# One row tile ahead of the expert rows instead of two: the order of a streaming encoder layer with gathered experts

## The reference, cut to what matters

```
h    = RMSNorm(x);  proj = h @ w_in            # 5416 columns: aq ak av, index, bq bk bv, 4 x 512 gate columns
oA   = attention over the top-k keys of an indexer;  oB = attention in a band with a bias
x    = x + (sig(gA) * (oA @ w_br_a) + sig(gB) * (oB @ w_br_b)) @ w_out
q    = RMSNorm(x) @ w_pq                       # 8 heads, two half keys each, against 128 + 128 centroids
e, g = 16 of 16384 experts per head and token, with softmax weights: 128 expert slots per token
x    = x + sum_k g_k * gelu(u[e_k] . h) * v[e_k]     # u, v: 16384 x 1024 (67 MB each)
```

## Time and profile before

| | before |
|---|---|
| time, median of 3 | 1466.76 us (1457.18 to 1469.15) |
| the profiled execution's own time | 1468.48 us |
| its span, first to last instruction | 1466.7 us |
| mean granted clock of TensorE | 0.841 of 2.4 GHz |
| busy: PE, DVE, ACT, POOL | 1168.0, 991.4, 294.8, 653.9 us |
| DMA moved | 434.92 MB |

### The profile page before, as it was taken

One profiled execution on the slowest core, in us unless ns is written; L12 is line 12 of the kernel. 1 busy time (PEld: TensorE's weight loads), 2 busy tenths in 40 slices (PEclk: granted clock), 3 DMA queues, 4 the chain that ended last, 5 costly groups with the idle time before them and its releaser, 6 DMA issues.

```text
span 1466.7 us, 12558 instructions
## 1 busy us (share of the span) xinstructions
PE 1168.0 (80%) x4129; PEld 695.6 (47%) x4129; DVE 991.4 (68%) x2233; ACT 294.8 (20%) x703; POOL 653.9 (45%) x565
## 2 busy tenths in 40 slices
PE   7999999798455664745778654277999999999998
PEld 3544544685125664635345654265444444444443
DVE  2526322487849998788768999998565666666662
ACT  2014631111000102111244643397000000000000
POOL 1220000265555556577646645556545454444450
PEclk9999999899775555555898876567999999999999
DMA  7643522398997778789999877676999999999994
GB/s 284 212 157 125 186 80 92 133 379 318 339 385 243 254 265 300 259 277 342 355 348 378 300 252 259 218 234 216 401 410 409 409 405 409 410 409 409 409 409 183
DMA packets 155362, 434.92 MB, mean 297 GB/s; under 512 B 14592, under 2 KB 36496, under 8 KB 155040
## 3 DMA queue, kind: packets, MB, share of 16 engines
q0 software_dynamic: 74688, 271.66, 50.7%
q1 hardware_dynamic: 80608, 162.45, 30.2%
HBM read 427.72 MB, written 6.34 MB: 296 GB/s over the span
## 4 chain that ended last, share of the span: by engine, by line
PE 57%; DVE 18%; DMA 11%; ACT 6%; another core or an unknown queue 4%; issue 2%; POOL 0%; SPq 0%; DVEq 0%; ACTq 0%
PE wide L1213 30%; PE accumB L896 8%; DVE rows_ring L1546 8%; PE accumA L896 5%; DMA arena<-in_w_in 3%; ACT hot L828 2%; PE wide L1103 2%; PE accumB L1125 2%; DVE arena L1534 2%; DMA ring<-in_w_in 2%; PE accumB L1159 1%; ACT hot L831 1%; DMA ring<-in_w_pq 1%; PE transB L1159 1%
## 5 line engine op out<-in xcount | busy, mean ns | idle before, releaser
L595 POOL DMA_INDIRECT rows_ring<-in_peer_u,expert x384 | 485.7, 1265 | 358.6 <-DVE dots L1546 277.6
L1546 DVE CUSTOM_DVE_ANT_0 rows_ring<-rows_ring,arena 128x1024 f32<-128x1024 f32 x384 | 459.3, 1223 | 108.3 <-DMA rows_ring<-in_peer_u,expert 105.4
L1213 PE MATMUL wide<-ring,arena 128*128 128x512 f32 x1024 | 441.9, 594 | 0.7 <-issue 0.7
L1213 PEld LDWEIGHTS wide<-ring,arena 128*128 128x128 f32 x1024 | 195.3, 191 | 246.8 <-issue 246.8
L1551 DVE SCALAR_TENSOR_TENSOR x<-rows_ring,dots,x 128x1024 f32<-128x1024 f32 x128 | 164.4, 1285 | 97.2 <-DMA rows_ring<-in_peer_v,expert 97.2
L595 POOL DMA_INDIRECT rows_ring<-in_peer_v,expert x128 | 125.1, 977 | 136.6 <-DVE x L1551 125.7
L872 PE MATMUL transB<-ident,arena 128*128 128x128 f32 x198 | 49.1, 392 | 81.4 <-DVE arena L1405 28.7
L896 PE MATMUL accumB<-arena 128*128 128x512 f32 x160 | 79.5, 654 | 26.0 <-DMA arena<-in_w_in 25.3
L896 PE MATMUL accumB<-ring,arena 128*128 128x512 f32 (+1 forms) x192 | 83.0, 587 | 12.3 <-DMA ring<-in_w_in 9.5
L828 ACT ACTIVATE hot<-iota,turned 128x128 f32<-128x128 f32 x256 | 81.0, 390 | 5.7 <-DVE expert L1504 5.7
L535 POOL TENSOR_SCALAR ssx<-ssx 128x1 f32<-128x1 f32 x6 | 2.0, 335 | 176.7 <-ACT arena L615 176.7
(11 more groups left out here) (215 smaller groups left out, 1376.5 us busy)
## 6 DMA issues: line engine op xcount, KB each, us to landing
ring<-in_peer_v SPq DMA_DIRECT2D x128, 512.0 KB
ring<-in_w_in SPq DMA_DIRECT2D x10, 2048.0 KB
arena<-in_w_in SPq DMA_DIRECT2D x10, 2048.0 KB
ring<-in_w_pq SPq DMA_DIRECT2D x4, 2048.0 KB
arena<-in_w_pq SPq DMA_DIRECT2D x4, 2048.0 KB
arena<-in_w_out SPq DMA_DIRECT2D x3, 2048.0 KB, 14.0
rows_ring<-in_peer_u,expert POOLq DMA_INDIRECT x384
arena<-in_w_br_a SPq DMA_DIRECT2D x2, 2048.0 KB
```

Source lines behind the costliest of these rows:

```text
L595: pool.indirect_dma_start(rowbuf[:, n % ROWS, :], None, u_rows if n < U_ROWS else v_rows, index).then_inc(S(f"rows{n % ROWS}"), 16)
L1213: ins = pe.matmul(wide[:, 2 * t + half, :], dense[t][:, b, :], vblock[:, b % VBLOCKS, half * 512:half * 512 + 512], start=b == 0, stop=b = ...
L1546: v.tensor_tensor_reduce(row, row, h2[:, t, :], 1.0, 0.0, ALU.mult, ALU.add, dots[:, t, k:k + 1]).then_inc(S("row_used"), 1)
```

## The change

The two Groups become three Lanes: A (tile 0, "first"), B (tile 1, "second") and C (sample). Ahead of the rows only lane A runs: projection, attention, gates, branches, output, queries (tables FIRST_*, in `before_rows`). Tiles 1 and 2 are projected together as a group GL ("late") between rows, from position 0.5 on; then B's attention, gates, branches, output and queries run between rows at positions 5 to 31, beside C's. Weights are thus loaded in three passes where there were two: the seven projection groups for A and for GL, the gates, branches, output and query weights for each of A, B and C. A's pass uses four ring slots, the others two. B has one transpose bank and one sum bank (transA, accumA), C the other two.

The dense matrix is laid out by token (`[p, token, block]`), so that a group of four tokens fills 512 contiguous floats, and ORDER names the sequence in which tile 0's groups are put, so that each goes where the arena is free already. In the last loop the stationary operand is now `dense[t][:, :, b]`, whose elements lie 128 floats (512 bytes) apart.

```
-PROJ = [4.5, 5.5, 6.5, 7.5, 8.5, 9.5, 10.5]
-GATES = [40.5, 41.5, 43, 44]
-AT = dict(heads_a=14, index=15, select=19.5, score_a=[18.5, 20.5, 21.5, 22.5], soft_a=24.5, values_a=[26.5, 27, 27.5, 28],
-          heads_b=25.5, score_b=[28.5, 30, 31.5, 33], soft_b=36, values_b=[38, 38.5, 39, 39.5], branch=[46, 47.5], merge=49,
-          out=[49.5, 51], scale=52, h2=53)
-QUERY = dict(prompt=[-8, -4, -3, -2, -1], sample=[53, 56, 59, 62])
-ROUTE = [[[-7, -7, -5, -5, -3, -3, 0]] + [route_at(2, 4), route_at(6), route_at(13.5)], [route_at(m) for m in (16.5, 21, 28.5, 42.5)],
-         [route_at(m) for m in (56, 59, 62, 65)]]
-DENSE = [(35, 46, 1.7), (67, 67.5, 4)]
+FIRST_PROJ = [9, 14, 21, 28, 35, 42, 49]
+FIRST_AT = dict(index_heads=27, index=34, heads_a=41, select=38, score_a=[48], soft_a=52, values_a=[57, 57, 57, 57],
+                heads_b=61, score_b=[70], soft_b=71, values_b=[87, 87, 87, 87], gates=[62, 71, 80, 98], branch=[91, 105],
+                merge=112, out=[114, 121], scale=130, h2=131, late=78, centroids=48.5, h_late=24)
+LATE_PROJ = [0.5, 1.5, 3, 4.5, 5.5, 7, 8.5]
+SECOND_AT = dict(index_heads=5, index=6, heads_a=7, select=7.5, score_a=[8], soft_a=9.5, values_a=[12.5, 13, 13, 13.5],
+                 heads_b=11.5, score_b=[12.5], soft_b=13.5, values_b=[15.5, 16, 16, 16.5],
+                 gates=[10, 11, 14, 14.5], branch=[17, 18.5], merge=20, out=[20.5, 22], scale=23.5, h2=24)
+SAMPLE_AT = dict(index_heads=5.5, heads_a=12, index=16.5, select=21, score_a=[21.5, 22.5, 23.5, 24], soft_a=26,
+                 values_a=[27.5, 28, 28.5, 29], heads_b=26.5, score_b=[29.5, 31, 32.5, 34], soft_b=36.5,
+                 values_b=[39.5, 40, 40, 40.5], gates=[33, 34.5, 36, 37], branch=[42, 43.5], merge=45, out=[46, 47.5],
+                 scale=49, h2=50)
+QUERY = dict(first=[-8, -4, -3, -2], second=[25, 27, 29, 31], sample=[50.5, 53, 55.5, 58])
+         [route_at(m) for m in (27.5, 31, 34.5, 39.5)],
+         [route_at(m) for m in (52.5, 55.5, 58.5, 61.5)]]
+DENSE = [(35, 44, 1.8), (64.5, 65, 4)]
+ORDER = [[28, 29, 30, 31] + list(range(8)) + list(range(12, 20)) + list(range(8, 12)) + [20, 21, 27] + list(range(22, 27)),
+         list(range(TGROUPS))]
...
+        LOADS = [("first", name, n % 4) for n, name in enumerate(NAMES7 + REST)]
+        LOADS += [("late", name, n % 2) for n, name in enumerate(NAMES7)]
+        LOADS += [(owner, name, (n + 1) % 2) for owner in ("second", "sample") for n, name in enumerate(REST)]
...
-                    act.activation(dense[t][:, :, g * TOKENS:g * TOKENS + TOKENS],
-                                   built[(g + 1) % 2][:, :].rearrange("p (n b) -> p b n", n=TOKENS),
+                    act.activation(dense[t][:, first:first + TOKENS, :],
+                                   built[(g + 1) % 2][:, :].rearrange("p (n b) -> p n b", n=TOKENS),
                                    ACT.Copy).then_inc(S("dense_put"), 1)
...
-            between = [laid(x) for x in (early(steps(G0)), queries(G0), steps(G1), dense_weights(0), queries(G1),
-                                         dense_weights(1))]
+            before_rows([laid(x) for x in (project(GF, FIRST_PROJ), attention(A), gates(A), finish(A))])
+            between = [laid(x) for x in (queries(A), project(GL, LATE_PROJ), attention(B), gates(B), finish(B),
+                                         attention(C), gates(C), finish(C), queries(B), dense_weights(0), queries(C),
+                                         dense_weights(1))]
...
-                        ins = pe.matmul(wide[:, 2 * t + half, :], dense[t][:, b, :],
+                        ins = pe.matmul(wide[:, 2 * t + half, :], dense[t][:, :, b],
                                         vblock[:, b % VBLOCKS, half * 512:half * 512 + 512],
```

More of the change, by code:

```diff
@@ L367, in laid @@
                 m = yield
-        def early(steps):
-            for k in steps:
-                yield FIRST if k >= 0 else k
         def start_laid(between):
@@ new lines, in _ @@
+            sp.wait_ge(to(GL, "h_ready"), 2)
+            sp.dma_start(gain[:, :], to_all_rows(i["g_ffn"])).then_inc(S("gain_in"), 16)
+            for n in range(4):
+                weights("first", f"pq{n}")
+            for name in ("ix", "aq"):
+                weights("late", name)
+            sp.wait_ge(to(A, "query_done"), 16)
+            sp.wait_ge(to(A, "score_done"), 4)
+            sp.dma_start(cik, i["cache_a_ik"][0].rearrange("b k d -> k b d")).then_inc(S("cik_in"), 16)
+            for name in ("ak", "av", "bq", "bk", "bv"):
+                weights("late", name)
@@ new lines, in gate_copies @@
+            def gate_copies(L):
+                for n, at in enumerate(AT[L.name]["gates"]):
+                    yield at + 0.5
+                    act.wait_ge(to(L, "gate_done"), n + 1)
+                    if L is C and n == 0:
+                        act.wait_ge(to(C, "logits_read"), 1)
+                        act.wait_ge(S("state_stored"), 16 * 15)
+                    bank = {"first": [sumB, sumB, sumA, sumA], "second": [sumA] * 4, "sample": [sumB] * 4}[L.name][n]
+                    act.activation(L.gates[:, n * 512:n * 512 + 512], bank, ACT.Sigmoid).then_inc(to(L, "gate_copied"), 1)
@@ L747, in steps @@
-                if G is G1:
-                    yield from groups(range(7, NG), [p + 1 for p in GATES])
-                yield AT["merge"]
-                for t in every:
-                    for half in range(2):
-                        copy_rows(G, "merged", t, half)
-                for t in every:
-                    yield LAST["out"] if t else AT["scale"]
-                    act.wait_ge(to(G, "x1_added"), 2 * t + 2)
-                    squares(G.tiles[t], 1)
-                    yield LAST["out"] if t else AT["h2"]
-                    for half in range(2):
-                        copy_rows(G, "h2", t, half)
@@ new lines, in finish @@
+            def finish(L):
+                at = AT[L.name]
+                for br in range(2):
+                    yield at["branch"][br]
+                    branch(L, br)
+                yield at["merge"]
+                pe.wait_ge(to(L, "merged_ready"), 1)
+                rows(L, "merged", L.merged)
+                for n in range(2):
+                    yield at["out"][n]
+                    weights_wait(pe, L.name, f"out{n}")
+                    if n == 0:
+                        pe.wait_ge(to(L, "transposes_copied"), batch(L, "merged", 1) + 1)
+                    if L is A and n == 1:
+                        pe.wait_ge(to(A, "gate_copied"), 4)
@@ L1253, in streams_apart, with norms @@
                                      src.rearrange("p (b j) -> p b j", j=NEW))
-            def steps(G):
-                every = range(G.n)
+            def norms(G, at):
                 g0, name = G.tiles[0], G.name
@@ L1437, in together @@
+            before_rows([laid(x) for x in (norms(GF, FIRST_NORM), bias_rows_out(), index_parts(A), attention(A),
+                                           finish(A))])
             def together(instructions, name="dve_step"):
@@ L1536, in dense_weights @@
                     signal(ins, "hot1_ready")
-            between = [laid(x) for x in (early(steps(G0)), route(0), route(1), steps(G1), route(SAMPLE), weights(0),
+            between = [laid(x) for x in (route(0), route(1), norms(GL, LATE_NORM), index_parts(B), index_parts(C),
+                                         attention(B), finish(B), attention(C), finish(C), route(SAMPLE), weights(0),
                                          dense_weights(0), weights(1), dense_weights(1), weights(SAMPLE))]
```

1578 lines of the change are left out of this document (807 added, 771 removed).

## The result

The changed kernel takes 1451.73 us (median of 4 runs, 1446.77 to 1455.88) against 1467.14 for the kernel before; the ratio is 0.9895 [0.9864, 0.9925]. Measured again beside the later experiments it was 1450.08 against 1471.22, ratio 0.9856 [0.9816, 0.9897]. So it is faster by 1.0 to 1.4%, where 3.6% were forecast. The profiled execution took 1450.86 us, its span 1449.0.

The account below looks back on a forecast made before the run. PE was taken to bound the prologue and last loop, DVE the two stages between, with DMA close. 179 + 320 + 468 = 967 us, plus 441.9 and 5.6, gave 1414 us; range 1350 to 1475.

Parts of the forecast that it names:

- last loop: Final part, bound by PE: starts at about 967 us with row 297 and takes 441.9 us.
- the size of the idle time around DVE's work: Both stages between rows: DVE's busy share before, 82% in stage 1 and 86% in stage 2, guided their lengths.
- stage 1: From the first gather to row 107: DVE work 250 us, length 320 us (bounds 290 and 360), before 278.
- stage 2: From row 107 to the last loop: DVE work 410 us, length 468 us (bounds 435 and 485), before 459.
- prologue: Up to the first gather: PE 135, first wait 8, gaps 20, route 16; 179 us (169 to 199), before 282.
- one new hold: SP's queue in stage 1: the sample's value cache waits for tile 1's values, holding query weights and other caches behind it.
- Stage 1's resources: Stage 1: DVE, DMA and PE near 290 us at once; DMA share above 0.92, clock above 0.71.
- Rival (b): Stage 1 takes the prologue's gain through extra loads and late PE: 360 us there, total 1474, no change; chance 0.20.
- The stretch before the last loop: End of stage 2: ACT's 32 groups at 2.3 us take 74 us; starting ten rows earlier saves 13 us of DVE.
- I take no cost: Last loop's strided weight loads stay hidden, up to 2.27 times 190 ns; cost bounds 0 and 338 us.
- rival (c): Last loop becomes bound by strided loads; beats the 52 us gain from 482 ns, total 1556 at 570 ns; chance 0.07.
- Rival (a): Moved work falls into DVE's idle time in both stages: 290 and 440 us, total 1357; chance 0.22.

Follow-up runs that it names:

- Experiment 1: Changed kernel with the sample's last two value-cache loads issued ahead of its two branch weights in SP's queue: 1436.86 us, ratio 0.9785 to the kernel before.
- experiment 6: Experiment 1's kernel with tile 1's third and fourth query weights also issued ahead of some of the sample's value caches: 1427.69 us, ratio 0.9746 to the kernel before.
- Experiment 4: Changed kernel with the positions of the sample's route and tile 1's dense weights as in the kernel before: 1468.28 us, ratio 0.9996 to the kernel before.
- experiment 7: Changed kernel with tile 1's dense weights block by block, ACT writing them float by float at a 512-byte step: 1463.90 us, ratio 0.9973 to the kernel before.
- experiment 10: Experiment 7's kernel with 128 instead of 512 columns behind each weight load of the last loop: 1697.41 us, ratio 1.1539 to the kernel before.
- experiments 2 and 3: Tile 1's last route quarter at position 42.5 instead of 39.5: on the changed kernel 1462.03 us, on Experiment 1's kernel 1451.10 us.

## Why the prediction was right and wrong

**The step that failed is the size of the idle time around DVE's work.** In the prediction: "DVE 395 becomes 410, at 86% 477 us ... I take 468 (bounds 435, no idle above 5% on DVE; 485)", and for stage 1 320 us on 250 of DVE. The work was right in both stages within 2 us. The idle time was sized by the busy share of the kernel before (86% in stage 2, 82% in stage 1). It turned out as 84% and 75%: 78 us idle where the forecast left 58, and 82 where it left 70, so 20 and 12 us more. The forecast was 37.7 us too low: 5 in the prologue, 11 in stage 1, 18 in stage 2, and the rest, 3, lies between the end of the span and the median.

**What stood in its place in stage 2 is shown:** loads held up by their place in SP's queue. Experiment 1 takes back 14 us of the last loop's start, and experiment 6 another 8 (6 by the ratios), with the same loads issued; after them stage 2 is 464 us, inside the bounds and 4 under the forecast. In the changed kernel it was 486, 1 us beyond the bound of 485 and 9 beyond the 477 that the share of the kernel before would have given. I had read SP's queue for the change and named one new hold (the value caches behind tile 1's values, "The first may show in PE"). I did not read on to the second: the load of the sample's rows waits for the sample's fourth gate, which the change had moved from behind the values to in front of them, and after it come the branch weights, then the last value caches. An item like that can be found without a run: for each load in the new queue, what it waits for, and who is waiting for it.

Of the 11 us in stage 1 nothing was tried. The trace has DVE waiting 47.5 us for rows from 184 to 515 and 12.2 us for tile 1's branch products (L1474), at a DMA share of 0.83. The idle time grew most there, from 50 us in the kernel before to 82. It stays open which of SP's loads, if any, stands in front.

**Prologue, 179 against 184, inside 169 to 199: right term by term.** PE's 155.4 us up to 184 are not all ahead of the first route, which starts at 169.6:

```profile
0.00:168.00 168.00, 139.80 (x462) 73.05 (x463) 48.08 (x103) 36.97 (x87) 19.28 (x34) 0.93 0.77 279
168.00:184.00 16.00, 15.63 (x139) 15.44 (x139) 12.55 (x65) 4.53 (x11) 0.20 (x1) 1.00 0.24 77
```

PE is busy 139.8 us up to 168, where I counted 135, and idle 28.2, where I gave 28 (8 and 20); the route and the first gather's issue take the last 16, as counted. The 15.6 us of PE beside the route are, but for the first quarter's last scores, the next queries' work, which the sum rightly left out.

**Stage 1's resources.** The DMA share was to be above 0.92; it was 0.83. PE was counted at 309 us, at best 270; it was 259, at a clock of 0.81 instead of 0.71. Neither was full over the stage as a whole; whether one was in parts of it stays open. Rival (b), by which the stage would eat the gain (360 us), did not come true in that form. What was left of the prologue's gain at row 107 was 45 us (forecast 61).

**The stretch before the last loop** was read rightly: it ends by ACT's 32 groups at 2.3 us, and it can start 10 rows sooner. Experiment 4 shows that without this, which took half a paragraph of the prediction, nothing of the gain is left, and experiment 7 agrees that the stretch is ACT's. I weighed it at 13 us of DVE's rows; taking it away cost 22 us of start and 17 of time.

**The last loop** started with row 296 (forecast 297) and took 442.1 us. "I take no cost" for the strided loads was right. The margin was argued wrongly: I set a record of 190 ns against 431 and gave the load 2.27 times. By experiment 10 the room is 0.22 us strided, so the margin is nearly twofold already with the step, and rival (c), which began at a *record* of 482 ns, was told by the wrong quantity. The Trainium skill's SBUF — State Buffer, in the note on cachelines under "Door 1: The DMA port swizzle", says that fewer than two hits to a 16-byte line cost bandwidth. Experiments 7 and 10 agree and give it sizes: a load takes twice the room or more, an ACT write 1.65 times as long.

**Rival (a)**, the moved work falling into idle time at 1357 us, asked for DVE over 90% busy. Even experiment 6 has 88% in stage 2.

## What to carry to other kernels

When work moves between positions, sort each DMA queue afterwards by when its loads are needed, and ask of each load in front of an urgent one what it waits for itself. A large load that nobody needs yet, in front of a small one that is needed now, delays it by its own transfer, and by more where other queues share the memory: here 4 MB, 10 us at 404 GB/s, came with a wait of 19.9. The DMA share of the stage doesn't show it; a slice at full rate followed by a nearly idle one did here.

A wait has a place where it is met and a place where it is made. Work that stands in front of the meeting place is cover. Moving it behind does not shorten the wait and leaves the work to be done after it, as experiments 2 and 3 show; there the wait even ended later. Look for the maker, three queues back here, and leave the cover.

When a kernel is rearranged and also retuned, undo the retuning alone: here, with two lines of positions put back, nothing of the gain was left.

## What the runs showed of the hardware

- In fp32 with 128 x 128 elements, a weight load's record is longer than the room the load takes. Contiguous: 192 ns of record at one load in 0.11 us. With a step of 512 bytes: 313 ns of record at one in 0.22 us. With 512 columns behind each load both were hidden; with 256 the last loop took 448.7 us instead of 442, so they were hidden but for 7 us at most.
- ACT writing 512 fp32 columns: 0.58 us in one run or in runs of four floats, 0.96 us float by float at a step of 512 bytes.
- Loads issued on SP's queue kept their order in effect: a 0.5 MB piece issued at 657.3, behind 4 MB issued 5 us before, came so late that PE went on at 683.9. The Trainium skill's DMA: Bandwidth & Descriptors, section "Queues, rings and completion order", says that each DMA engine takes a ring's descriptors in order. Experiment 1 agrees: the same piece, issued at 662.6 ahead of the weights, made no wait that the list of PE's waits shows.
